# Expert stage of a streaming encoder step: the order in which a token list's entries are laid on the partitions

## The chip, the cores and the metric

The kernel runs on one core of a Trainium2 chip. The metric is the device time of one execution in microseconds. The kernel before was run three times: 1291.88, 1288.03 and 1289.56 us, median 1289.56 us. One more execution was taken with the hardware profiler; all rows below come from it.

## What is computed

The program is one layer of an encoder over 1024 prompt rows and 32 sample rows of width 1024: projections, two kinds of attention, an output projection, and then a mixture of 32 gated experts. Only the mixture bears on this change. Each of the 1056 rows picks one of four groups and two of the eight experts in it, so there are 2112 pairs of a row and an expert:

```python
g_sel = jnp.argmax(g_logits, axis=-1)
e_in = jnp.take_along_axis(e_logits, g_sel[:, None, None], axis=1)[:, 0]
top_v, top_i = lax.top_k(e_in, TOP_K)                       # TOP_K = 2
w2 = jax.nn.softmax(top_v, axis=-1) * p_g
idx = g_sel[:, None] * EXP_PER_GROUP + top_i
gates = jnp.einsum('ske,sk->se', jax.nn.one_hot(idx, N_EXPERTS), w2)
a = jnp.einsum('sd,edf->sef', hs, w_gate)                   # 1024 -> 256, for each expert
b = jnp.einsum('sd,edf->sef', hs, w_up)
act = jax.nn.silu(a) * b * gates[:, :, None]
return jnp.einsum('sef,efd->sd', act, w_down)               # 256 -> 1024
```

Working the routing out from the reference's own inputs gives how many rows each expert gets: between 37 and 107, 66 on average. These counts are used below. In the kernel's order of experts (four fixed ones, then 14 of the two middle groups by falling count, "busy", then 14 of the other two groups, "calm") they are 69, 70, 37, 47; busy 101, 94, 84, 78, 75, 74, 72, 67, 66, 61, 56, 54, 48, 46; calm 107, 92, 86, 80, 78, 73, 70, 63, 49, 47, 47, 42, 41, 38.

## The kernel before

Phase F (`phase_fr`) normalises and routes, and writes for each expert a list in device memory (`list_dram`, a region of rows for each expert): entry after entry, a row's number and its weight, 8 bytes together. Behind the last real entry stand padding entries whose number is out of bounds.

Phase G (`phase_g`) works in 23 blocks of 128 partitions. A block holds one expert (128 places), two experts with 64 places each, or 96 places of one expert and 32 of a fourth one that three such blocks share. `expert_blocks` makes this plan: for each block, pieces of (expert, first entry, places, first partition). Blocks 0, 1, 2 and 4 are the fixed experts; 3, 11, 13, 15 and 22 are pairs; 12 and 14 single experts; 5 to 10 and 16 to 21 are two and two groups of "four experts in three blocks".

For each block:
- a small DMA for each piece loads its entries of the list into `li[b]`, entry j on partition j of the piece. Lists 0 and 1 are loaded by SyncE at the end of phase F (L1879), the others by ScalarE (`list_in`, L2579), seven blocks' lists in a row at the start of phase G and then one block's list after each block, nine blocks ahead;
- GpSimd issues an indirect DMA that gathers the rows named in `li[b]` from `h2_dram` into one of four buffers (`gather`, L2389; the tiles `g_xg`, `early` and `o_s`), 4 KB for each partition; out-of-bounds entries are skipped;
- TensorE turns the rows (L2396), multiplies them by gate and up (L2404, 16 to 64 matmuls), turns the hidden rows (L2411) and multiplies them by down (L2419);
- VectorE scales the result by the entry's weight (L2632), and GpSimd issues an indirect DMA that adds the rows to the output `y` in device memory (`scatter`, L2383), 4 KB for each real entry. It waits for the scatter before it.

The weights, 3 MB for each of the other 28 experts, come in 1 MB DMAs issued by SyncE (`load_gate_up`, `load_down`, L2278 to L2284) into six slots; a slot is loaded again when TensorE has done with it. All DMAs of the core, whoever issues them, run on its 16 DMA engines. In `first_products` TensorE waits for the block's gate and up weights; the profile names no releaser for this wait and calls it "issue".

The order of the instructions on each engine is written out by hand in the program; no scheduler decides it.

Of the kernel before, what the change touches and what calls it, by code (L numbers as in the profile page):

```python
# [31 lines left out]
P = 128  # L32
D = 1024
KD = D // P
SEQ, DEC, PAST = 1024, 32, 2048
# [13 lines left out]
NG, EPG, NE, DE = 4, 8, 32, 256  # L49
# [1704 lines left out]
def phase_fr(nc, io, g):  # L1754

    with ExitStack() as stack:
# [85 lines left out]
        @block.sync  # L1842
        def _(sp):
            def rows_in(n):
                i, T, side = tile(n)
                if n >= 2:
                    sp.wait_ge(x2_done, n - 1)
                src = io["x_sample"] if side else io["x_prompt"][i * P:(i + 1) * P, :]
                sp.dma_start(xr[0:T, n % 2], src).then_inc(x_in[n % 2], 16)

            rows_in(0)
            rows_in(1)
            sp.dma_start(wr[:, :, 0:NG], io["w_rg"].rearrange("(k p) n -> p k n", p=P)).then_inc(r_in, 16)
            sp.dma_start(wr[:, :, GW:], io["w_re"].rearrange("(k p) n -> p k n", p=P)).then_inc(r_in, 16)
            sp.wait_ge(pad_done, 1)
            sp.dma_start(g.list_dram.rearrange("(p n) o -> p n o", p=P), pad[:]).then_inc(z_out, 16)
            for n in range(NT):
                i, T, side = tile(n)
                sp.wait_ge(x2_done, n + 1)
                sp.dma_start(io["y"][i * P:i * P + T, :], x2[0:T, n % 2]).then_inc(st_x2[n % 2], 16)  # L1860
                if n + 2 < NT:
                    rows_in(n + 2)
                sp.wait_ge(h2_done, n + 1)
                sp.dma_start(g.h2_dram[i * P:i * P + T, :], h2[0:T]).then_inc(st_h2, 16)
                if n in (1, 2, 6):
                    q = min(n - 1, 2)
                    load_gate_up(nc, io, g, sp, q * EPG, q, g.wgu_in[q])
                    load_down(nc, io, g, sp, q * EPG, q, g.wd_in[q])
            sp.wait_ge(pr_mm, NT)
            load_gate_up(nc, io, g, sp, 3 * EPG, 3, g.wgu_in[3])  # L1870
            load_down(nc, io, g, sp, 3 * EPG, 3, g.wd_in[3])
            sp.wait_ge(st_h2, 16 * NT)
            for b in range(2):
                sp.wait_ge(st_x2[b], 16 * len(range(b, NT, 2)))
            for b in range(2):
                sp.wait_ge(listed[b], 32 * len(range(b, NT, 2)))
            for b in range(2):
                row = b * EPG * REGION
                sp.dma_start(g.li[b][:], g.list_dram[row:row + P, :]).then_inc(g.li_in[b], 16)  # L1879

        @block.gpsimd
        def _(pool):
# [401 lines left out]
    engine.dma_start(g.w_down[b][:], io["w_down"][e].rearrange("(p k) n -> p k n", p=P)).then_inc(sem, 16)  # L2284


def expert_blocks():

    busy = lambda r: FIXED + r
    calm = lambda r: FIXED + RANKS + r  # L2290

    def whole(p):
        return [(p, 0, P, 0)]

    def halves(p, q):
        return [(p, 0, P // 2, 0), (q, 0, P // 2, P // 2)]

    def four_in_three(three, shared):
        w = 3 * P // 4
        return [[(p, 0, w, 0), (shared, i * DEC, DEC, w)] for i, p in enumerate(three)]  # L2300

    single = [whole(p) for p in (busy(0), calm(0))]
    paired = [halves(busy(r), calm(r)) for r in range(THREE, RANKS)]
    fours = []
    for r in range(WHOLE, THREE, 4):
        fours.append(four_in_three([busy(r), busy(r + 1), busy(r + 2)], calm(r + 3)))
        fours.append(four_in_three([calm(r), calm(r + 1), calm(r + 2)], busy(r + 3)))
    fixed = [whole(p) for p in range(FIXED)]
    blocks = fixed[0:3] + paired[0:1] + fixed[3:4] + fours[0] + fours[1] + paired[1:2] + single[0:1] + paired[2:3]
    return blocks + single[1:2] + paired[3:4] + fours[2] + fours[3] + paired[4:5]  # L2310


def phase_g(nc, io, g):

    with ExitStack() as stack:
# [7 lines left out]
        order = []  # L2323
        first_block, last_block = {}, {}
        for b in range(NB):
            for p, _, _, _ in blocks[b]:
                if p not in first_block:
                    order.append(p)
                    first_block[p] = b
                last_block[p] = b  # L2330
# [95 lines left out]

        def slots_of(b):

            unit = min(n for _, _, n, _ in blocks[b])
            return [place[p] for p, _, n, _ in blocks[b] for _ in range(n // unit)]  # L2430

        @block.sync
        def _(sp):
# [70 lines left out]
        @block.tensor  # L2504
        def _(pe):
            def first_products(b):
                for p, _, _, _ in blocks[b]:
                    pe.wait_ge(wgu_in[place[p]], 32 * nth[p] + 32)
                pe.wait_ge(xT_done, b + 1)
                if b:  # L2510
                    pe.wait_ge(hid_done, b)
                gate_up(b % 2, slots_of(b)).then_inc(gu_mm, 1)

            def rows_turned(b):
                pe.wait_ge(xg_in[b % ROWSETS], 16 * (b // ROWSETS) + 16)
                if b:
                    pe.wait_ge(xT_done, b)
                transposes(b % ROWSETS).then_inc(xT_mm, 1)

            def second_products(b):  # L2520
                for p, _, _, _ in blocks[b]:
                    pe.wait_ge(wd_in[place[p]], 16 * nth[p] + 16)
                pe.wait_ge(hT_done, b + 1)
                if b >= 2:
                    pe.wait_ge(y_done, b - 1)
                down(b % 2, slots_of(b)).then_inc(dn_mm, 1)

            def hidden_turned(b):
                pe.wait_ge(hid_done, b + 1)
                if b:  # L2530
                    pe.wait_ge(hT_done, b)
                hid_transposes().then_inc(hT_mm, 1)

            rows_turned(0)
            rows_turned(1)
            for b in range(NB + 1):
                if b == NB - 1:
                    second_products(b - 1)
                if b < NB:
                    first_products(b)  # L2540
                if b and b != NB - 1:
                    second_products(b - 1)
                if b + 2 < NB:
                    rows_turned(b + 2)
                if b < NB:
                    hidden_turned(b)

            def long_body(e, row, n):
                pe.wait_ge(l_xg, n * 16 + 16)
                transposes(0).then_inc(l_xT_mm, 1)  # L2550
                pe.wait_ge(l_xT, n + 1)
                pe.wait_ge(l_w, n * 48 + 48)
                gate_up(0, [0]).then_inc(l_gu, 1)
                pe.wait_ge(l_hid, n + 1)
                hid_transposes().then_inc(l_hT_mm, 1)
                pe.wait_ge(l_hT, n + 1)
                down(0, [0]).then_inc(l_dn, 1)

            long_lists(pe, long_body)

        @block.scalar
        def _(act):
            def squash():
                return nc.scalar.activation(sig[:], GU[:, 0:DE], ACT.Sigmoid)  # L2564

            def hidden_out(b):
                return nc.scalar.activation(hT[:, b], H[:, 0:FT * P].rearrange("p (k t) -> p k t", t=P), ACT.Copy)  # L2567

            AHEAD = 9
            experts = {r: r * EPG for r in range(FIXED)}  # L2570

            def expert(r):
                if r not in experts:
                    experts[r] = act.value_load(g.order[0:1, r:r + 1], min_val=0, max_val=NE - 1)
                return experts[r]

            def list_in(b):
                for r, row, n, at in blocks[b]:
                    act.dma_start(li[b][at:at + n, :], g.list_dram[bass.ds(expert(r) * REGION + row, n), :]  # L2579
                                  ).then_inc(li_in[b], 16)  # L2580

            act.wait_ge(xg_in[0], 16)
            for b in range(2, AHEAD):
                list_in(b)
            for b in range(NB):
                act.wait_ge(gu_mm, b + 1)
                if b:
                    act.wait_ge(hid_done, b)
                squash().then_inc(sig_done, 1)
                act.wait_ge(hT_mm, b + 1)  # L2590
                if b >= 2:
                    act.wait_ge(dn_mm, b - 1)
                hidden_out(b % 2).then_inc(hT_done, 1)
                if b + AHEAD < NB:
                    list_in(b + AHEAD)

            def long_body(e, row, n):
                act.wait_ge(l_gu, n + 1)
                squash().then_inc(l_sig, 1)
                act.wait_ge(l_hT_mm, n + 1)  # L2600
                hidden_out(0).then_inc(l_hT, 1)

            long_lists(act, long_body)
# [238 lines left out]
```

## Time and profile before

| | us |
|---|---|
| median of three runs | 1289.56 (1288.03 to 1291.88) |
| the profiled execution, from its first to its last instruction | 1289.9 |
| TensorE (PE) busy in it | 1182.8 (92%) |
| VectorE (DVE) busy | 672.3 (52%) |
| ScalarE (ACT) busy | 356.3 (28%) |
| GpSimd (POOL) busy | 212.8 (16%) |
| bytes moved by DMA | 213.47 MB, 165 GB/s over the span |
| expert stage, from the landing of the first lists to the end | 970.5 to 1289.9 |

The span of the profiled execution lies 0.3 us above the median of the runs. The page cuts the span into 40 slices of 32 us and gives for each the busy share of each engine, the clock granted to TensorE, and the mean busy share of the 16 DMA engines. A stretch can be asked for the same numbers. The chain of work that ended last lists, in order of time, what each piece of the critical path was.

### The profile page before, as it was taken

What the parts mean: (1) busy time and instruction counts of PE and PEld (TensorE: products, weight loads), DVE (VectorE), ACT (ScalarE), POOL (GpSimd) and SP (SyncE); (2) the same over time, 40 slices, a digit from 0 to 9 for tenths busy, and PEclk for the clock granted to TensorE, in tenths of its full rate; (3) what the DMA queues carried; (4) which work ended last, traced back from release to release, by engine and by line L of the source; (5) the groups of instructions that cost most, each with busy time, mean ns of one, the idle gap of its engine ahead of it and who ended that gap; (6) DMA issues with size and microseconds to landing.
All of it is one profiled execution on the core that took longest, in us unless ns stands there. A gap on an engine that the chain in (4) does not pass through costs nothing. (4 is left out here: it accounts for less than half of the span.)

```text
span 1289.9 us, 19011 instructions
## 1 busy us (share of the span) xinstructions
PE 1182.8 (92%) x7174; PEld 662.3 (51%) x7175; DVE 672.3 (52%) x1313; ACT 356.3 (28%) x781; POOL 212.8 (16%) x250
## 2 busy tenths in 40 slices
PE   4999999999978997899999999899976999977995
PEld 1555555555543556666677776555543433332331
DVE  1255443554465884567777775544462554433443
ACT  1122222222222444265555553323320000000000
POOL 4000000000000002254443322011022212211111
PEclk9899999999998998889999999899977999988998
DMA  8721211111137871421111005362447999999993
GB/s 361 297 66 33 66 53 46 53 45 54 41 122 226 300 275 58 124 58 30 29 29 30 2 1 165 121 231 89 184 152 285 337 367 367 382 395 377 357 348 65
DMA packets 92834, 213.47 MB, mean 165 GB/s; under 512 B 20673, under 2 KB 54707, under 8 KB 77394
## 3 DMA queue, kind: packets, MB, share of 16 engines
q1 hardware_dynamic: 82258, 195.02, 41.1%
q0 software_dynamic: 7200, 17.33, 5.4%
q8 instruction: 53, 0.87, 0.3%
q10 hardware_dynamic: 3296, 0.02, 0.1%
q14 instruction: 27, 0.22, 0.1%
HBM read 185.03 MB, written 34.13 MB: 170 GB/s over the span
## 5 line engine op out<-in xcount | busy, mean ns | idle before, releaser
L2404 PE MATMUL g_GU<-w_gu,first_region 128*32 128x512 f32 (+2 forms) x656 | 143.0, 624 | 17.0 <-issue 17.0
L1921 PE MATMUL f_C<-first_region,oT 128*128 128x512 f32 x256 | 115.2, 603 | 0.0
L454 PE MATMUL U<-region,b_hT 128*128 128x512 f32 x256 | 112.3, 592 | 0.0
L2614 DVE TENSOR_TENSOR g_sig<-g_GU,g_sig 128x256 f32<-128x256 f32 x23 | 9.8, 425 | 165.8 <-ACT g_sig L2564 157.7
L1723 DVE TENSOR_TENSOR_SCAN region<-region,early 128x128 f32<-128x128 f32 (+7 forms) x64 | 88.6, 1404 | 6.3 <-POOL region L1530 6.3
L2404 PEld LDWEIGHTS g_GU<-w_gu,first_region 128*32 128x32 f32 (+2 forms) x656 | 43.2, 127 | 84.3 <-issue 83.4
L454 PE MATMUL b_UL<-region,b_hT 128*128 128x384 f32 (+1 forms) x256 | 76.5, 458 | 3.3 <-DMA region<-w_in 3.3
L1921 PEld LDWEIGHTS f_C<-first_region,oT 128*128 128x128 f32 x256 | 48.0, 193 | 54.3 <-issue 54.2
L454 PEld LDWEIGHTS U<-region,b_hT 128*128 128x128 f32 x256 | 47.5, 190 | 54.2 <-issue 54.0
L2383 POOL DMA_INDIRECT y<-oT,g_li x23 | 36.4, 1584 | 227.0 <-DVE oT L2632 133.8
L1592 PE MATMUL e_Z<-first_region,region 104*128 104x512 f32 (+3 forms) x192 | 70.8, 507 | 0.1
L2419 PE MATMUL g_Y<-w_down,early 128*32 128x512 f32 (+2 forms) x328 | 68.8, 594 | 0.7 <-ACT early L2567 0.7
L1538 POOL TENSOR_SCALAR region<-region,e_sm 128x128 f32<-128x128 f32 (+7 forms) x64 | 47.0, 745 | 130.1 <-DVE e_sm L1736 130.1
L454 PEld LDWEIGHTS b_UL<-region,b_hT 128*128 128x128 f32 x256 | 49.9, 196 | 31.1 <-issue 5.5
L1052 POOL MEMSET region<- 128x256 f32 x1 | 0.3, 311 | 375.2 <-POOLq L303 375.2
L1729 DVE TENSOR_REDUCE e_sm<-e_Z 128x1 f32<-128x128 f32 (+7 forms) x64 | 46.4, 745 | 21.7 <-PE e_Z L1592 20.8
L2564 ACT ACTIVATE g_sig<-g_GU 128x256 f32<-128x256 f32 x23 | 8.8, 383 | 175.3 <-PE g_GU L2404 175.3
L454 PE MATMUL b_U<-region,b_hT 128*128 128x512 f32 x128 | 56.3, 592 | 0.0
L1685 ACT ACTIVATE region<-e_Z,e_sm 128x128 f32<-128x128 f32 (+7 forms) x64 | 47.2, 749 | 11.5 <-DVE e_sm L1729 11.4
L2404 PE MATMUL g_GU<-first_region 128*32 128x512 f32 (+2 forms) x144 | 49.4, 594 | 0.0
L1592 PEld LDWEIGHTS e_Z<-first_region,region 104*128 104x128 f32 x192 | 34.0, 199 | 29.3 <-issue 26.2
L1663 ACT ACTIVATE region<-e_Z 128x128 f32<-128x128 f32 (+7 forms) x64 | 38.1, 649 | 34.8 <-PE e_Z L1574 34.8
(489 smaller groups left out, 2160.2 us busy)
## 6 DMA issues: line engine op xcount, KB each, us to landing
w_gu<-w_gate SPq DMA_DIRECT2D x21, 1024.0 KB
w_gu<-w_up SPq DMA_DIRECT2D x21, 1024.0 KB
w_down<-w_down SPq DMA_DIRECT2D x21, 1024.0 KB
region<-w_ada SPq DMA_DIRECT2D x16, 1024.0 KB, 7.0
region<-w_in SPq DMA_DIRECT2D x3, 2048.0 KB, 17.5
oT<-w_gate SPq DMA_DIRECT2D x6, 1024.0 KB
oT<-w_up SPq DMA_DIRECT2D x6, 1024.0 KB
oT<-w_down SPq DMA_DIRECT2D x6, 1024.0 KB, 20.2
```

Of the source, the lines that this page charges most:

```text
L454: end = nc.tensor.matmul(dst[0:T, 0:c1 - c0], lhsT=hT[:, k, 0:T], rhs=g.w_in[:, k, c0:c1], start=k == 0, stop=k == KD - 1)
L1538: nc.gpsimd.tensor_scalar(part, part, sm[:, n % 2, 4 + hh:5 + hh], 1.0, ALU.mult, ALU.mult).then_inc(scaled, 1)
L1592: end = nc.tensor.matmul(Z[:, hh, at + c:at + c1], lhsT=g.q_hidden[:, b, h, :], rhs=g.kT_hidden[:, h, c:c1], start=True, stop=True)
L1663: nc.scalar.activation(stick[:, n % 2, hh, 0:W], Z[:, hh, at:at + W], ACT.Tanh, scale=0.5 * SB_SCALE).then_inc(tanh_done, 1)
L1685: nc.scalar.activation(w[:, hh, to:to + W], Z[:, hh, at:at + W], ACT.Exp, bias=sm[:, n % 2, hh:hh + 1], accum_out=sm[:, n % 2, 2 + hh:3 + ...
L1723: nc.vector.tensor_tensor_scan(back, back, least, 1.0, ALU.mult, ALU.max).then_inc(scan_done, 1)
L1729: nc.vector.tensor_reduce(sm[:, n % 2, hh:hh + 1], Z[:, hh, at:at + (t + 1) * P], AX.X, ALU.max, negate=True).then_inc(max_done, 1)
L1921: end = nc.tensor.matmul(C[n % 2][:, c * 512:(c + 1) * 512], lhsT=g.oT[:, i, k, :], rhs=wo[:, k, c * 512:(c + 1) * 512], start=k == 0, sto ...
L2383: nc.gpsimd.indirect_dma_start(out=io["y"][:, :], in_=rows, in_offset=None, out_offset=bass.IndirectOffsetOnAxis(ap=li[:, 0:1], axis=0), b ...
L2404: end = nc.tensor.matmul(GU[h * n:h * n + n, :], lhsT=xT[:, b, k, h * n:h * n + n], rhs=wgu[s][:, :, k, :], start=k == 0, stop=k == KD - 1 ...
L2419: end = nc.tensor.matmul(Y[b][h * n:h * n + n, c * 512:(c + 1) * 512], lhsT=hT[:, b, k, h * n:h * n + n], rhs=wd[s][:, k, c * 512:(c + 1) ...
L2614: mark(nc.vector.tensor_tensor(sig[:], GU[:, 0:DE], sig[:], ALU.mult))
```

## The change

The pieces get one more number, the step between the list's entries that they take, and every list is read through a new helper.

```diff
+def list_rows(g, row, first, step, n):
+
+    rows = g.list_dram[bass.ds(row, n * step), :].rearrange("(r q s) c -> s q r c", r=8, s=step)
+    return rows[first]
...
     def whole(p):
-        return [(p, 0, P, 0)]
+        return [(p, 0, 1, P, 0)]
 
     def halves(p, q):
-        return [(p, 0, P // 2, 0), (q, 0, P // 2, P // 2)]
+        return [(p, 0, 1, P // 2, 0), (q, 0, 1, P // 2, P // 2)]
 
     def four_in_three(three, shared):
         w = 3 * P // 4
-        return [[(p, 0, w, 0), (shared, i * DEC, DEC, w)] for i, p in enumerate(three)]
+        return [[(p, 0, 1, w, 0), (shared, i, 3, DEC, w)] for i, p in enumerate(three)]
...
-                for r, row, n, at in blocks[b]:
-                    act.dma_start(li[b][at:at + n, :], g.list_dram[bass.ds(expert(r) * REGION + row, n), :]
+                for r, first, step, n, at in blocks[b]:
+                    act.dma_start(li[b][at:at + n, :], list_rows(g, expert(r) * REGION, first, step, n)
                                   ).then_inc(li_in[b], 16)
```

The load of lists 0 and 1 at the end of phase F goes through `list_rows` too, with step 1 and 128 entries. For a piece with n places the helper reads the list as 8 stretches of n/8 entries and takes the first of each stretch, then the second of each, and so on: entry j goes to partition 8 * (j mod n/8) + j div (n/8) of its piece. Consecutive entries land eight partitions apart. A shared expert with places in three blocks gives its entries 0, 3, 6, ... to the first of them, 1, 4, 7, ... to the second and 2, 5, 8, ... to the third; before, they got entries 0 to 31, 32 to 63 and 64 to 95.

The destination of each load is the same; the source is read as (n/8) x 8 x 2 numbers, so its outermost dimension is 16, 12, 8 or 4 where it was 128, 96, 64 or 32. No instruction is added, taken away or moved. On ScalarE, at the start of phase G (lists of block 2, of the two halves of block 3, and of block 4; the ISA rows are register work for the expert's address), stood before:

```order
L2579 DMA g_li<-list_dram 128x2
L2574 TENSOR_LOAD order
L2574 ISA x2
L2579 ISA
L2579 DMA g_li<-list_dram 64x2
L2574 TENSOR_LOAD order
L2574 ISA x2
L2579 ISA
L2579 DMA g_li<-list_dram 64x2
L2579 DMA g_li<-list_dram 128x2
```

and now stands, in the same place:

```order
L2584 DMA g_li<-list_dram 128x1x2
L2579 TENSOR_LOAD order
L2579 ISA x2
L2584 ISA
L2584 DMA g_li<-list_dram 64x1x2
L2579 TENSOR_LOAD order
L2579 ISA x2
L2584 ISA
L2584 DMA g_li<-list_dram 64x1x2
L2584 DMA g_li<-list_dram 128x1x2
```

Only the form of the DMAs differs, and the line numbers by five.

## Rows read from the trace of the kernel before

**Rows 1.** The page: DMA share (tenths) and GB/s in 40 slices of 32 us

```profile
DMA  8721211111137871421111005362447999999993
GB/s 361 297 66 33 66 53 46 53 45 54 41 122 226 300 275 58 124 58 30 29 29 30 2 1 165 121 231 89 184 152 285 337 367 367 382 395 377 357 348 65
```

**Rows 2.** Stretches of the expert stage: busy by engine, granted clock, DMA share, GB/s

```profile
core 0: us, PE busy (x) PEld busy (x) DVE busy (x) ACT busy (x) POOL busy (x), PEclk, DMA share, GB/s
1000.00:1040.00 40.00, 40.00 (x158) 18.33 (x160) 21.39 (x31) 2.68 (x7) 7.92 (x6) 1.00 0.93 334
1040.00:1180.00 140.00, 129.63 (x845) 49.60 (x838) 56.64 (x85) 8.05 (x21) 28.86 (x22) 0.95 1.02 379
...
1139.90:1144.00 4.10, 4.00 (x10) 1.38 (x12) 0.00 (x0) 0.00 (x0) 0.00 (x0) 0.50 1.02 357
```

**Rows 3.** The waits between 1100 and 1240 us, TensorE: total, times, longest

```profile
PE g_GU L2404 <- issue: 17.0, 4, 7.3
```

**Rows 4.** The chain that ended last, in the expert stage: start, us, what

```profile
968.79 1.69 DMA g_li<-list_dram
...
1120.87 6.87 PE g_GU L2404 x16
...
1132.65 7.34 issue
1139.99 9.68 PE g_GU L2404 x32
...
1166.21 3.03 issue
1169.24 8.72 PE g_GU L2404 x32
...
1182.72 5.17 issue
1187.89 9.61 PE g_GU L2404 x64
...
1202.41 7.00 PE g_GU L2404 x64
...
1225.94 1.46 issue
```

**Rows 5.** The last scatter (84 rows, nothing else moves), in stretches of 0.3 us

```profile
1284.90:1285.20 0.30, 0.00 (x0) 0.00 (x0) 0.00 (x0) 0.00 (x0) 0.00 (x0) 0.50 1.02 205
1285.20:1285.50 0.30, 0.00 (x0) 0.00 (x0) 0.00 (x0) 0.00 (x0) 0.00 (x0) 0.50 0.95 164
1285.50:1285.80 0.30, 0.00 (x0) 0.00 (x0) 0.00 (x0) 0.00 (x0) 0.00 (x0) 0.50 0.50 83
1285.80:1286.10 0.30, 0.00 (x0) 0.00 (x0) 0.00 (x0) 0.00 (x0) 0.00 (x0) 0.50 0.37 69
1286.10:1286.40 0.30, 0.00 (x0) 0.00 (x0) 0.00 (x0) 0.00 (x0) 0.00 (x0) 0.50 0.35 68
1286.40:1286.70 0.30, 0.00 (x0) 0.00 (x0) 0.00 (x0) 0.00 (x0) 0.00 (x0) 0.50 0.34 68
```

**Rows 6.** The first two gathers (69 and 70 rows), same columns

```profile
974.00:975.00 1.00, 0.00 (x0) 0.00 (x0) 0.00 (x0) 0.00 (x0) 0.63 (x1) 0.50 0.57 201
```

**Rows 7.** Around the gather of block 2, TensorE and VectorE in order of time

```profile
990.57 1.16 PE L2396 MATMUL g_X<-ident,early 128*128 128x128 f32 x8 [0.73 <-DMA early<-h_dram,g_li]
991.57 0.40 PE L2411 MATMUL g_H<-ident,g_hid 128*128 128x128 f32 x2
...
1002.11 1.05 PE L2396 MATMUL g_X<-ident,o_s 128*128 128x128 f32 x8
```

```profile
990.75 0.42 DVE L2615 TENSOR_TENSOR g_hid<-g_GU,g_sig 128x256 f32<-128x256 f32 x1
```

**Rows 8.** GpSimd in order of time: gathers of blocks 2 to 4, first scatter

```profile
981.47 0.99 POOL L2389 DMA_INDIRECT early<-h_dram,g_li  x1 [6.84 <-DMA g_li<-list_dram]
...
985.60 0.99 POOL L2389 DMA_INDIRECT o_s<-h_dram,g_li  x1 [2.16 <-DMA g_li<-list_dram]
989.17 0.99 POOL L2389 DMA_INDIRECT g_xg<-h_dram,g_li  x1 [2.57 <-DMA g_li<-list_dram]
...
1004.70 1.62 POOL L2383 DMA_INDIRECT y<-oT,g_li  x1 [6.51 <-DVE oT L2632]
```

**Rows 9.** The page: DMA queue of ScalarE's list loads: packets, MB, share

```profile
q10 hardware_dynamic: 3296, 0.02, 0.1%
```

More of the change, by code:

```diff
@@ L1877, in _ @@
             for b in range(2):
-                row = b * EPG * REGION
-                sp.dma_start(g.li[b][:], g.list_dram[row:row + P, :]).then_inc(g.li_in[b], 16)
+                sp.dma_start(g.li[b][:], list_rows(g, b * EPG * REGION, 0, 1, P)).then_inc(g.li_in[b], 16)
         @block.gpsimd
@@ L2325, in phase_g @@
         for b in range(NB):
-            for p, _, _, _ in blocks[b]:
+            for p, *_ in blocks[b]:
                 if p not in first_block:
@@ L2427, in slots_of @@
         def slots_of(b):
-            unit = min(n for _, _, n, _ in blocks[b])
-            return [place[p] for p, _, n, _ in blocks[b] for _ in range(n // unit)]
+            unit = min(n for _, _, _, n, _ in blocks[b])
+            return [place[p] for p, _, _, n, _ in blocks[b] for _ in range(n // unit)]
         @block.sync
@@ L2506, in first_products @@
             def first_products(b):
-                for p, _, _, _ in blocks[b]:
+                for p, *_ in blocks[b]:
                     pe.wait_ge(wgu_in[place[p]], 32 * nth[p] + 32)
@@ L2520, in second_products @@
             def second_products(b):
-                for p, _, _, _ in blocks[b]:
+                for p, *_ in blocks[b]:
                     pe.wait_ge(wd_in[place[p]], 16 * nth[p] + 16)
```

## The prediction, written before the changed kernel was run

> **What bounds the kernel now.** The page's slices come first, because the change touches DMAs alone. Before the expert stage the DMA engines are mostly idle; from slice 31 to slice 39 they stand at 9 tenths and move 337 to 395 GB/s [rows 1]. Next come stretches of that stage. From 1000 to 1040 us the DMA share is 0.93 and TensorE has no gap; from 1040 to 1180 us the share is 1.02, so that all 16 DMA engines have work all the time, and TensorE is busy 129.63 of 140 us [rows 2]. The waits say where the rest goes: TensorE stands four times, 17.0 us in all, ahead of gate-and-up products [rows 3], and the code has a wait for weights there. The chain gives the places: 7.34 us at 1132.65 (block 13), 3.03 us (block 15), 5.17 us (block 16) and 1.46 us at 1225.94 (block 19) [rows 4]. The products behind the three long waits take 9.68, 8.72 and 9.61 us where the others take 6.87 to 7.00: after the first of them the granted clock is 0.50 up to 1144 us, 1.2 of 2.4 GHz [rows 2]. Another 2.7 + 1.7 + 2.6 = 7.0 us. So up to 24 us of this stage hang on DMA, and outside these places it runs at TensorE's pace.
>
> A wait for weights ends when the last of the 16 DMA engines has done its part. A weight load gives each engine the same; a gather or a scatter doesn't, since it skips padding. What counts is how many rows fall to the engine that gets most, in each block: its "depth". Lowering that is the only way in which this change can reach those 24 us.
>
> **Which engine moves which partition.** Nothing names it, but the last scatter shows it, because nothing else moves then. Block 22 holds 46 rows on partitions 0 to 45 and 38 rows on 64 to 101. Had each engine eight consecutive partitions, 46 = 5 x 8 + 6 and 38 = 4 x 8 + 6 rows would keep 11 engines busy, a share of 0.69 to the end. The rows show 1.02 and 0.95, then 0.50, 0.37, 0.35, 0.34 [rows 5]: all 16 engines, then six (0.375). That fits groups of four partitions, dealt in turn to eight engines in each half of the partitions: 12 groups in the first half are one for each engine and a second for four, 10 groups in the second half are one each and a second for two; 4 + 2 = 6. An engine then has partitions 4e to 4e + 3 and the four that lie 32 further on. The first gathers, 69 and 70 rows, run at a share of 0.57 [rows 6]: some nine engines of 16.
>
> The Trainium skill says the same of the shares ("DMA: Bandwidth & Descriptors", The descriptor swizzle: four consecutive partitions and the four that lie 32 on). It speaks against this change as much as the rows do; the sum doesn't need it.
>
> **The change part by part.** (1) *Entries eight partitions apart.* With 128 places, entry j lands on partition 8 (j mod 16) + j div 16. Entries 0 to 63 fill the first four places of each eight, so they all lie in every second group of four, and these groups go to every second engine. Those eight engines get 8 rows each, the other eight only what is over 64. Before, entries 0 to 63 lay on the first 64 partitions: eight engines with 8 rows each. The idle engines are other ones, the depth is 8 both times. The same count for 64 places: entries 0 to 31 fill four engines with 8 each. For 96 places entries 0 to 47 fill every second group in the same way. Going through the 23 blocks with the lists' lengths, the depth is 8 in all of them before, and 8 in 21 after; only blocks 2 (37 rows) and 4 (47 rows) fall to 6. Over the stage the deepest engine has 184 rows before and 180 after, where an even spread would give 132.
>
> What those two blocks are worth: block 2's gather is on the path at the start, since TensorE stands 0.73 us for it [rows 7]. But the hidden rows that are turned behind it at 991.57 come from VectorE at 990.75 + 0.42 = 991.17, so at most some 0.4 us can be won; I take 0.3. A scattered row costs a DMA engine: 69 GB/s at a share of 0.37 is 69 / (0.37 x 16) = 11.7 GB/s for one engine, 4096 bytes in 0.35 us [rows 5]. A gathered row: 201 / (0.57 x 16) = 22 GB/s, 0.19 us [rows 6]. Block 4's scatter falls behind 1040 us, where the engines are saturated: 2 x 0.35 = 0.7 us from each later wait for weights. The other rows (block 2's gather and scatter, block 4's gather) fall ahead of 1040 us, where TensorE doesn't wait; if they count after all it is 2 x 0.35 + 4 x 0.19 = 1.5 us more. Taken: -0.7, bounds 0 and -2.2.
>
> (2) *The shared expert's entries in turn.* Of 78, 75, 49 and 66 entries, the blocks get 26/26/26, 25/25/25, 17/16/16 and 22/22/22 where they got 32/32/14, 32/32/11, 32/17/0 and 32/32/2. This evens out blocks' totals, but the 96 other places already put 8 rows on some engine in each of the 12 blocks. 0 us.
>
> (3) *The list loads.* Each still carries its n entries of 8 bytes, read with a stride. The first two lists landed in 1.69 us [rows 4] with eight entries an engine; that stays. For the shorter loads the trace can't show what a source with an outermost dimension of 12, 8 or 4 does. If each were spread over that many engines, the first four would hold 16 list entries for a pair or four-in-three block where they held 8: 17 blocks x 8 = 136 more. Priced by the queue's own row, 0.1% (0.05 to 0.15) of 16 x 1289.9 us over 3296 packets is 3 to 9 ns each [rows 9], so 0 to +1.2 us on one of the deepest engines; eight of the 17 blocks' lists are loaded after 1040 us, 64 x 6 ns = 0.4 us, which I take. At the start the lists arrive 3.6 to 4.1 us apart, at 981.47, 985.60 and 989.17 [rows 8]. If a pair's takes twice that, block 3's gather starts at 989.4; a gather there takes 9.05 us at most (981.47 to 990.52), and TensorE wants it at 1002.11 [rows 7], so it may start as late as 993. The first scatter stands behind the gathers on GpSimd's queue and would come at some 1009 for 1004.70 [rows 8]; VectorE wants its end two blocks on, after 1025. Nothing on the path.
>
> The skill does state a rule on this ("DMA: Bandwidth & Descriptors", Why a DMA increments its semaphore by 16 and not by 1): the number of engines is the largest one up to 16 that divides the slowest dimension of both sides, and it is the lowest-numbered ones. By it the loads run on 16, 12, 8 and 4 engines; no row of this trace shows it. The sum by it is the +0.4 us taken, and without it 0.
>
> (4) *More engines at the same depth.* One engine had 8 rows in every block; now all of every second one have, but for two blocks. A wait for the last of eight is a little longer than one for the last of three or four: 0 to +1 us, I take +0.3, about one row's packet.
>
> Sum: -0.3 - 0.7 + 0 + 0.4 + 0.3 = -0.3 us on a span of 1289.9 us, which lies 0.3 us above the median of the runs. The forecast is 1289.3 us: no change that can be measured. About 0.3%, 3.9 us, is what a measurement of this kernel can tell from none.
>
> **The rivals.** *A: the rows are evened out after all.* If each engine took eight consecutive partitions in gathers and in scatters under load, transposed lists would give each the ceiling of rows/16. By block 19's weights the deepest engine would save 14 scattered rows of blocks 4 to 15 (96 to 82) and 19 gathered rows of blocks 10 to 22 (104 to 85): 14 x 0.35 + 19 x 0.19 = 8.5 us, all of it out of the 24 us. That is 1289.6 - 8.5 = 1281 us, and some 1278 if shorter waits also spare the clock. For it: depth is what the waits hang on. Against it: the six engines of rows 5, which eight consecutive partitions can't give. *B: slower, by the list loads.* Same spreading as in (3), but each entry costs an engine more than its packet time, since it is a read of its own that stands between 8 KB packets. It decides from 3.9 / 64 = 0.06 us an entry on. The dearest row is the 1.69 us of a load with eight entries deep, 0.21 us each with all latency in it [rows 4]; half-way, 0.12 us, gives 64 x 0.12 = +8 us, 1297 us; at the bound it is 1303. Against it: 3 to 9 ns [rows 9].
>
> **How the numbers follow.** The forecast holds 0.82, rival A 0.09, rival B 0.09. Within the forecast the bounds of the parts are -0.4 - 2.2 = -2.6 and +1.2 + 1.0 = +2.2 us; with 2 us for the spread of the runs (1288.03 to 1291.88) that is 1285.2 to 1293.8. This leaves out the two rivals, 0.18, so it is the range. Of the forecast's 0.82, some 0.04 lie beyond the 3.9 us on the fast side and 0.03 on the slow side: faster 0.13, same 0.75, slower 0.12.
>
> **What would show it.** In the profile after: the last scatter falls from a share of 1 to about 0.5 (eight engines) half-way instead of 0.37, and ends as late; the waits for weights at blocks 13, 15, 16 and 19 stay, 15 to 18 us in all; the wait of 0.73 us for block 2's gather is gone. Rival A shows as a last scatter of even share to the end and as waits under 10 us. Rival B shows as longer waits and list loads that land much later. The number of packets on the list loads' queue tells of (3): it falls if loads end on fewer engines. What would make the prediction wrong above all is that the engines are dealt the partitions in another way under load than in the last scatter.

## The result: 1301.34 us for 1290.72, slower by 0.8%

| | median (lowest to highest) | ratio to before, 95% interval | span profiled |
|---|---|---|---|
| before, beside it | 1290.72 us (1288.03 to 1292.56) | 1 | 1289.9 us |
| changed kernel | 1301.34 us (1299.28 to 1302.86) | 1.0081 (1.0061 to 1.0100) | 1301.2 us |

The forecast was 1289.3 us, no change, with a range up to 1293.8. The time lies 12.0 us above the forecast and outside the range. The profiled execution of the changed kernel took 1302.85 us, one of its slower ones, with a span of 1301.2 us. The two spans lie 0.1 and 0.8 us below the medians and can stand for the runs.

The stage still ends as it did: the chain that ended last runs through TensorE, and its waits for weights have hardly moved. The waits and the two windows of [rows 2] come first; in a row of waits stand the engine, the line and what it waits for, then the total, the times and the longest. First the waits between 1100 and 1240 us of the changed kernel, then two stretches of it with busy time by engine, granted clock, DMA share and GB/s:

```profile
PE g_GU L2409 <- issue: 18.1, 4, 6.8
```

```profile
1000.00:1040.00 40.00, 40.00 (x127) 18.68 (x126) 17.30 (x25) 2.69 (x7) 7.30 (x6) 0.94 0.70 246
1040.00:1180.00 140.00, 129.80 (x858) 50.36 (x858) 60.70 (x88) 8.45 (x22) 30.35 (x24) 0.97 1.01 377
```

Beside [rows 3] that is 18.1 us for 17.0, and beside [rows 2] the saturated 140 us are the same stretch again: 129.80 us of TensorE for 129.63, share 1.01 for 1.02. What differs is the stretch ahead of it. Only 127 products ran from 1000 to 1040 us where 158 did, at a granted clock of 0.94 where it was 1.00. Nearly all of the 11 us is lost before 1040 us, as the chain shows. Pieces of the chain of the changed kernel (start, us, what), to be read against [rows 4]:

```profile
975.34 0.69 ACTq L2584
...
1000.37 9.22 PE g_GU L2409 x16
...
1143.39 6.78 issue
1150.17 9.55 PE g_GU L2409 x32
...
1176.25 3.42 issue
...
1192.89 5.44 issue
```

The wait at block 13 begins at 1143.39 for 1132.65, 10.74 us later; nearly all of the loss is there by then. From 975.34 to 997 us the chain leads through something that [rows 4] doesn't have: ACTq, ScalarE's own queue, at the line that loads the lists. ScalarE in order of time (start, us, engine, line, operation, count, idle time before and its releaser), of the kernel before:

```profile
975.66 11.41 ACTq L2579 DMA_DIRECT2D g_li<-list_dram  x12
987.10 1.28 ACT L2564 ACT_TABLE_LOAD   x1 [26.19 <-issue]
989.88 0.38 ACT L2564 ACTIVATE g_sig<-g_GU 128x256 f32<-128x256 f32 x1 [1.49 <-PE g_GU L2404]
```

and of the changed kernel:

```profile
975.34 21.65 ACTq L2584 DMA_DIRECT2D g_li<-list_dram  x12
997.02 1.28 ACT L2569 ACT_TABLE_LOAD   x1 [36.70 <-issue]
998.32 0.38 ACT L2569 ACTIVATE g_sig<-g_GU 128x256 f32<-128x256 f32 x1
```

ScalarE issues twelve list loads, for blocks 2 to 8, ahead of the stage's first sigmoid. They took 11.41 us; they take 21.65 us. Before, ScalarE had done with them and with its table and then waited 1.49 us for TensorE. Now the sigmoid stands behind them without any gap. Who waits for that sigmoid is in TensorE's own rows of the changed kernel:

```profile
989.35 1.06 PE L2401 MATMUL g_X<-ident,early 128*128 128x128 f32 x8
999.67 0.70 PE L2416 MATMUL g_H<-ident,g_hid 128*128 128x128 f32 x2 [9.26 <-DVE g_hid L2620]
```

TensorE stands 9.26 us for the hidden rows that VectorE makes from this sigmoid. The gate-and-up products of block 1, right behind, take 9.22 us for 6.87: a window of the changed kernel shows the clock there.

```profile
1000.30:1005.00 4.70, 4.70 (x7) 1.89 (x6) 0.45 (x1) 0.38 (x1) 0.99 (x1) 0.50 0.47 158
```

The granted clock is 0.50, 1.2 of 2.4 GHz, behind a gap of 9.26 us; before, without the gap, these products began at 991.81. In all: the sigmoid comes 27.38 us after the start of the first gather (970.94 to 998.32) where it came 18.57 us after it (971.31 to 989.88), 8.81 us more; 9.22 - 6.87 = 2.35 us for the clock; waits of 18.1 for 17.0, 1.1 us. That is 12.3 us. The slowed products behind the long waits give 0.7 back (9.55 + 8.45 + 9.34 for 9.68 + 8.72 + 9.61), and the first gather starts 0.37 us sooner in the span (970.94 for 971.31). So 11.2 us, where the spans differ by 11.3 and the medians by 10.6.

What one load costs the queue is in the rows of the tile: shortest, median and longest issue in ns, first and last start. Of the kernel before, then of the changed one:

```profile
L2579 ACTq DMA_DIRECT2D g_li<-list_dram x38: 322/362/998, 975.7 to 1156.4; - x38
```

```profile
L2584 ACTq DMA_DIRECT2D g_li<-list_dram x38: 580/1116/1319, 975.3 to 1167.5; - x38
```

The number of loads is the same, 38; only the way in which the source is read has changed. The issues are not the whole of it. Between the loads of the start ScalarE reads the number of the next expert eight times, and these reads take longer too. Before, then changed, same columns:

```profile
L2574 ACTq TENSOR_LOAD <-order x8: 275/290/479, 976.1 to 986.0; - x8
```

```profile
L2579 ACTq TENSOR_LOAD <-order x8: 476/605/820, 976.1 to 995.0; - x8
```

Added up over the instructions of the traces, the twelve issues take 12.43 us for 4.74 and the eight reads 5.01 for 2.49: 7.7 and 2.5 us of the 10.24 by which the row of twelve grew.

### The profile page after: what moved, and what is told of

Its sections match the earlier page's. It is cut to its first block and busy times, and to the rows that moved or that the text cites. A ratio compares the mean times of both kernels' runs of the same rounds, so it can differ in the third digit from the quotient of the medians.

```text
span 1301.2 us, 19011 instructions
## 1 busy us (share of the span) xinstructions
PE 1184.0 (91%) x7174; PEld 663.3 (51%) x7175; DVE 672.3 (52%) x1313; ACT 356.3 (27%) x781; POOL 212.8 (16%) x250
## 5 line engine op out<-in xcount | busy, mean ns | idle before, releaser
L2409 PE MATMUL g_GU<-w_gu,first_region 128*32 128x512 f32 (+2 forms) x656 | 144.7, 625 | 18.1 <-issue 18.1
```

The source lines that it names most:

```text
L2409: end = nc.tensor.matmul(GU[h * n:h * n + n, :], lhsT=xT[:, b, k, h * n:h * n + n], rhs=wgu[s][:, :, k, :], start=k == 0, stop=k == KD - 1 ...
```

## The experiments

The theory (Q): the loss is ScalarE's time for issuing list loads, ahead of the first sigmoid. Its first rival (D) is the prediction's rival B: the loads' entries hold up the DMA engines between weights. The second (M) is the new mapping itself, by which blocks draw more engines and rows. The kernel before was run again beside the experiments: its median is 1290.2 us beside e2, e3, e4 and e7, and 1290.3 us beside e5, e6, e8 and e9.

**e2: six blocks' lists ahead instead of nine.** The changed kernel, with the loads of blocks 2 to 5 only ahead of the first sigmoid (lists 0 and 1 come from SyncE as before); the others follow one block at a time. The loads, their mapping and their entries are the same.

```diff
-            AHEAD = 9
+            AHEAD = 6
```

> The changed kernel, but ScalarE loads the lists of blocks 2 to 5 (6 DMAs) ahead of its first sigmoid, not those of blocks 2 to 8 (12 DMAs). Theory 1 (the strided list loads take ScalarE's queue 0.6 to 1.3 us each, where they took 0.3 to 0.6, and twelve of them stand ahead of the first sigmoid): the six end at about 985.6 us, the first sigmoid starts at 989.9 again, behind TensorE's first products, and the time is that of the kernel before, 1289 to 1292 us. Theory 2 (the entries fall on few DMA engines, so lists, gathers or weights arrive late): the same entries on the same engines, the time stays at 1300 to 1303 us.

Measured: 1291.62 us (1288.88 to 1293.94), ratio 1.0011 (1.0000 to 1.0023). The loss is gone. ScalarE of this kernel, in order of time:

```profile
973.71 10.25 ACTq L2584 DMA_DIRECT2D g_li<-list_dram  x6
983.99 1.28 ACT L2569 ACT_TABLE_LOAD   x1 [25.31 <-issue]
987.88 0.39 ACT L2569 ACTIVATE g_sig<-g_GU 128x256 f32<-128x256 f32 x1 [2.61 <-PE g_GU L2409]
```

Six loads take 10.25 us, ScalarE waits for TensorE again, and the sigmoid comes 18.58 us after the start of the first gather (969.30), as in the kernel before. All 38 loads are there, as dear as in the changed kernel (median 1114 ns), and more of them fall where the DMA engines are saturated: the last one starts at 1203.5 us. If entries on the DMA engines were the cost (D), or the mapping (M), this kernel would be no faster than the changed one.

**e7 and e8: the delay alone, in the kernel before.** Small copies on ScalarE into a tile that nothing reads, between the loads and the first sigmoid; lists and mapping stay those of before.

```diff
+        idle = m.sb("g_idle", [P, 36 * 32])
...
+            for n in range(36):
+                nc.scalar.activation(idle[:, n * 32:n * 32 + 32], g.gate_m[:, 0, 0:32], ACT.Copy)
```

> The kernel before with its lists as they were, and 36 small copies on ScalarE (some 0.23 us each, 8 us together) between the list loads and the first sigmoid. Theory 1: a late first sigmoid alone costs what the change cost; the sigmoid starts at about 996 to 998 us, the first products behind it run at the lower clock, and the time is 1298 to 1302 us. Theory 2: ScalarE's time is not what counts, 1289 to 1292 us.

The 36 copies took about half of what was meant, 4.40 us, and the time stayed under the 1298 to 1302 us expected. So the second run has 76 copies, of 16 columns each.

> As the run with 36 small copies ahead of the first sigmoid, with 76 of them; one took 0.12 us there, so the sigmoid starts at 987.1 + 76 x 0.12 + 1.3 = 997.5 us, 0.8 us ahead of the changed kernel's 998.3. Theory 1: the products behind it start 7.7 us late and run some 2 us longer at the lower clock, 1299 to 1301.5 us with lists as before. If it stays at the 1294.7 us of the short delay, a late sigmoid explains only half of the loss.

Measured: e7 1294.74 us (1292.07 to 1296.41), ratio 1.0032 (1.0020 to 1.0045); e8 1300.20 us (1298.09 to 1303.43), ratio 1.0076 (1.0058 to 1.0095). ScalarE of e8:

```profile
987.37 8.14 ACT L2587 ACTIVATE g_idle<-gate_m 128x16 f32<-128x16 f32 x76 [25.98 <-issue]
...
996.81 0.38 ACT L2565 ACTIVATE g_sig<-g_GU 128x256 f32<-128x256 f32 x1
```

| | first gather to first sigmoid | later than before | block 1's products | time over before |
|---|---|---|---|---|
| before | 18.57 us | | 6.87 us | |
| e7 | 21.52 us | 2.95 us | 8.56 us | 4.5 us |
| e8 | 25.11 us | 6.54 us | 8.59 us | 9.9 us |
| changed kernel | 27.38 us | 8.81 us | 9.22 us | 10.6 us |

A late first sigmoid is enough to make the kernel before slower by about as much as the changed one. The first 3 us cost 4.5 because the gap also brings the granted clock down for the products behind it (0.63 from 994.40 to 999.00 us in e7; 8.56 us for 6.87, +1.7). In e8 the delay and the clock explain 6.54 + 1.72 = 8.3 of the 9.9 us; its profiled execution also waits 19.3 us for weights, 2.3 more than before, and is the slowest of its four runs, so how much of the rest is scatter stays open.

The waits for weights don't take the delay back in any of the three, because the loads of weights start later too. The first weight load that waits for block 0's down products to free a slot stands in SyncE's rows; of the kernel before, then of the changed one:

```profile
1002.31 0.33 SPq L2284 DMA_DIRECT2D w_down<-w_down  x1
```

```profile
1013.06 0.33 SPq L2283 DMA_DIRECT2D w_down<-w_down  x1
```

That is 10.75 us later, as much as the wait at block 13 moved. In e7 this load starts at 1006.45 and in e8 at 1010.92.

**e6: the shared expert's entries in turn, alone.** The kernel before; the three 32-place pieces of a shared expert read entries 0, 3, 6, ..., 1, 4, 7, ... and 2, 5, 8, ..., everything else as it was.

```diff
-        return [[(p, 0, w, 0), (shared, i * DEC, DEC, w)] for i, p in enumerate(three)]
+        return [[(p, 0, w, 0), (shared, i, DEC, w)] for i, p in enumerate(three)]
...
+                    if at == 3 * P // 4:
+                        src = g.list_dram[bass.ds(expert(r) * REGION, 3 * n), :].rearrange("(q s) c -> s q c", s=3)[row]
```

> One part of the change alone: a shared expert's entries go to its three blocks in turn, all lists untransposed. The source of these loads keeps 32 as its outermost dimension, so by theory 1 their issue stays near 0.33 us and the first sigmoid at 990 us; the depth of rows stays 8. 1289 to 1292 us, waits for weights 16 to 19 us. If it takes half of the 10 us, the loss is in the shared pieces and not in the transposed lists.

Measured: 1289.74 us (1287.76 to 1293.20), ratio 1.0000 (0.9990 to 1.0011). The tile's row of this kernel:

```profile
L2582 ACTq DMA_DIRECT2D g_li<-list_dram x38: 322/364/636, 974.6 to 1156.1; - x38
```

The 0 us of the prediction's part (2) stands, and a stride between 32 entries by itself doesn't make a load dear: the outermost dimension is still 32.

**e3: entries four partitions apart.** The changed kernel with one number changed; consecutive entries then land in successive groups of four partitions, which by [rows 5] are different engines.

```diff
-    rows = g.list_dram[bass.ds(row, n * step), :].rearrange("(r q s) c -> s q r c", r=8, s=step)
+    rows = g.list_dram[bass.ds(row, n * step), :].rearrange("(r q s) c -> s q r c", r=4, s=step)
```

> The changed kernel with entries four partitions apart (4 stretches of n/4 entries, outermost dimension 32, 24, 16 or 8). By the reading of the last scatter (groups of four partitions dealt to the DMA engines in turn) this evens out the rows: the deepest engine has 150 rows for 184, and by block 19's weights it is 12 to 19 rows of each kind less, 7.3 us. The late first sigmoid stays. Theory 1: 1301 - 7 to 9, and up to 1.5 us less if the issue of a load is dear only where its outermost dimension spreads over fewer than 16 engines (then the loads of 64 places take 0.6 us again): 1291 to 1295 us, waits for weights under 12 us for 18.1. If partitions were dealt to engines eight by eight, the waits would stay at 18 us and the time at 1300.

Measured: 1288.99 us (1287.21 to 1292.25), ratio 0.9988 (0.9975 to 1.0001), 12.4 us faster than the changed kernel and hardly faster than before. Two things meet. The loads ahead of the first sigmoid, with the register work between them, still take 20.16 us for 21.65, the sigmoid comes 25.07 us after the first gather's start, 6.50 later than before, and block 1's products take 8.54 us: 6.50 + 1.67 = 8.2 us lost. Against that, the waits between 1100 and 1240 us of this kernel are

```profile
PE g_GU L2409 <- issue: 11.1, 4, 5.2
```

5.9 us less than [rows 3], and the products behind the long waits take 7.09 + 9.32 + 8.77 = 25.2 us for 28.0. Sum -0.5 us; the medians say -1.2. The run is 2 us faster than its expectation, which began at 1291: the waits and the products behind them gave more than the 7.3 us counted (beside the changed kernel 7.0 and 2.2 us).

**e4: four apart, six ahead.** Both edits.

> Both edits: entries four partitions apart, and only four blocks' lists ahead of the first sigmoid. Theory 1: the first sigmoid at 989.9 us as before, and waits for weights shorter by 7 us: 1281 to 1285 us, faster than both kernels. Theory 2: 1291 to 1295 us, no better than with nine blocks ahead.

Measured: 1282.02 us (1280.76 to 1285.10), ratio 0.9942 (0.9919 to 0.9964). This beats both kernels. Its waits between 1100 and 1240 us, then two pieces of its chain:

```profile
PE g_GU L2409 <- issue: 13.6, 3, 5.5
```

```profile
1126.90 2.72 issue
1129.62 7.09 PE g_GU L2409 x32
```

Against e2, which differs in the mapping alone, the medians are 9.6 us apart. The waits are 13.6 for 19.3 us (-5.7), the products behind the three longest 25.5 for 27.2 us (-1.7), and the start of the stage to the first sigmoid 16.41 for 18.58 us (-2.2: the first gather takes 3.50 us for 4.39, block 0's products 7.52 for 8.80). That adds up to the 9.6, but such agreement is partly luck: the profiled spans differ by 10.5 us, 1.3 of them ahead of the first gather (967.96 for 969.30), and the waits of kernels at the same depth scatter by 2.5 us (16.8 to 19.3 us). Its last scatter shows what the mapping does, in stretches of 0.3 us with the columns of [rows 5]; first e4, then the changed kernel:

```profile
1275.10:1275.40 0.30, 0.00 (x0) 0.00 (x0) 0.00 (x0) 0.00 (x0) 0.00 (x0) 0.50 0.99 178
1275.40:1275.70 0.30, 0.00 (x0) 0.00 (x0) 0.00 (x0) 0.00 (x0) 0.00 (x0) 0.50 1.00 191
1275.70:1276.00 0.30, 0.00 (x0) 0.00 (x0) 0.00 (x0) 0.00 (x0) 0.00 (x0) 0.50 0.80 150
1276.00:1276.30 0.30, 0.00 (x0) 0.00 (x0) 0.00 (x0) 0.00 (x0) 0.00 (x0) 0.50 0.28 41
```

```profile
1296.00:1296.30 0.30, 0.00 (x0) 0.00 (x0) 0.00 (x0) 0.00 (x0) 0.00 (x0) 0.50 0.98 110
...
1296.90:1297.20 0.30, 0.00 (x0) 0.00 (x0) 0.00 (x0) 0.00 (x0) 0.00 (x0) 0.50 0.57 109
...
1297.80:1298.10 0.30, 0.00 (x0) 0.00 (x0) 0.00 (x0) 0.00 (x0) 0.00 (x0) 0.50 0.55 109
```

Four apart, all engines carry nearly the same and the scatter is over at once. Eight apart, about half of them carry the rest alone, for longer. The groups of four that the prediction read from [rows 5] hold for gathers and scatters in the loaded part too: counted with them, the deepest engine has 150 rows over the stage where it had 184 before and 180 in the changed kernel, worth 7.3 us up to block 19 by the prediction's prices of a row, and the waits with their slowed products gave 7.4 between e2 and e4 and 7.3 between e2 and e9. The step is clear of the scatter: the seven kernels whose depth is nearly 8 throughout (184 or 180 rows) waited 16.8 to 19.3 us, the three evened ones 11.1, 13.6 and 14.0.

**e5: six ahead in the kernel before.** The same one-line edit as e2, so that its worth isn't put down to the wrong part.

> The kernel before with four blocks' lists ahead of the first sigmoid for seven, nothing else. Control for the two runs with that edit: before, ScalarE was free at 988.4 us and the sigmoid waited for TensorE until 989.88, so this should give nothing, 1289 to 1291.5 us. If it is faster by 2 us or more, part of what the other two runs gained is not the cure of a late sigmoid.

Measured: 1290.62 us (1289.74 to 1295.30), ratio 1.0006 (0.9991 to 1.0020). With loads of 0.37 us ScalarE's queue is not on the path there: the first sigmoid waits for TensorE in the kernel before, and with fewer loads ahead it only waits longer (7.12 us for 1.49). What e2 wins back is what the strided loads had cost, and the gain of e4 over before is the mapping's.

**e9: every load on an outermost dimension of 16 or a multiple, six ahead.** Groups chosen by size: 128 places four apart, 96 places six apart, 64 four apart, 32 two apart.

```diff
-    rows = g.list_dram[bass.ds(row, n * step), :].rearrange("(r q s) c -> s q r c", r=8, s=step)
+    rows = g.list_dram[bass.ds(row, n * step), :].rearrange("(r q s) c -> s q r c", r={P: 4, 3 * P // 4: 6, P // 2: 4, DEC: 2}[n], s=step)
...
-            AHEAD = 9
+            AHEAD = 6
```

> Lists transposed with 4 stretches for 128 and 64 places, 6 for 96 and 2 for 32, so that the outermost dimension is 32 or 16 for all, and six blocks ahead. If the issue of a list load is dear where the outermost dimension doesn't hold 16, all loads now take 0.55 to 0.7 us (1.28 us for 96 places and 1.15 for 32 before), against theory 1b, that the stride alone makes them dear, by which 96 places stay at 1.28 us. The rows are nearly as even (153 on the deepest engine, 46.7 us by block 19 for 46.1): 1280 to 1284 us, equal to the best one.

Measured: 1282.79 us (1280.63 to 1283.99), ratio 0.9942 (0.9929 to 0.9956), the same as e4. The tile's row of e9:

```profile
L2584 ACTq DMA_DIRECT2D g_li<-list_dram x38: 552/590/687, 974.5 to 1197.3; - x38
```

No load takes more than 687 ns any more. It brings no time over e4, since with six ahead the queue is off the path in both (the sigmoid waits 4.55 and 2.90 us for TensorE); it tells what makes a load dear. The single issues at the start of the stage, each one row of ScalarE in order of time (piece of 64, of 96 and of 32 places), of the changed kernel:

```profile
977.22 1.16 ACTq L2584 DMA_DIRECT2D g_li<-list_dram  x1
...
982.17 1.32 ACTq L2584 DMA_DIRECT2D g_li<-list_dram  x1
...
984.44 1.17 ACTq L2584 DMA_DIRECT2D g_li<-list_dram  x1
```

of e3:

```profile
973.73 0.61 ACTq L2584 DMA_DIRECT2D g_li<-list_dram  x1
...
977.04 1.38 ACTq L2584 DMA_DIRECT2D g_li<-list_dram  x1
...
979.33 1.22 ACTq L2584 DMA_DIRECT2D g_li<-list_dram  x1
```

and of e9:

```profile
976.35 0.60 ACTq L2584 DMA_DIRECT2D g_li<-list_dram  x1
...
979.66 0.62 ACTq L2584 DMA_DIRECT2D g_li<-list_dram  x1
...
980.99 0.61 ACTq L2584 DMA_DIRECT2D g_li<-list_dram  x1
```

The outermost dimensions of the three are 8, 12 and 4 in the changed kernel; 16, 24 and 8 in e3; 16, 16 and 16 in e9. The piece of 64 falls from 1.16 to 0.61 us when it goes from 8 to 16. The piece of 96 stays at 1.38 with 24 and falls to 0.62 with 16. So it isn't the number as such, nor how far apart the entries lie (12 or 24 apart the piece of 96 is dear, 16 apart it isn't): a load is cheap where the outermost dimension lets it run on 16 engines.

The other way round it doesn't always hold. The pieces of 32 places of blocks 6 and 7 in the changed kernel, on 4 engines as well, are nearly as cheap as in e9:

```profile
988.32 0.70 ACTq L2584 DMA_DIRECT2D g_li<-list_dram  x1
...
991.72 0.66 ACTq L2584 DMA_DIRECT2D g_li<-list_dram  x1
```

Eight of its twelve pieces of 32 places take 0.66 to 0.70 us, the other four 1.14 to 1.19. The cheap ones start within 0.5 us of the end of the load before; ahead of the dear ones stands the read of an expert's number, and they start 0.9 us or more behind it. e2, e3 and e4 show the same split. Why the spacing matters, no run shows.

## Why the prediction was wrong

**The step that failed is (3), the list loads.** It priced what each load does once it is under way: its landing, its entries on the DMA engines. It never priced the issuing. The document ahead of it says that ScalarE loads seven blocks' lists in a row at the start of the stage, and the queue's own time was to be had from the trace of before: 11.41 us for twelve loads, with 1.49 us of slack behind them. A term "twelve loads by an unknown more each, minus the slack" was missing. From 1.49 / 12 = 0.12 us a load the slack is used up, and with the 2.35 us for the clock (3.9 + 1.49 - 2.35) / 12 = 0.25 us a load decide the case. It was 10.24 / 12 = 0.85 us with the reads between the loads, and 10.24 - 1.49 = 8.75 us is the delay of 8.81 us. "Nothing on the path" was true for GpSimd's gathers, which step (3) followed (block 3's gather was put at 989.4 and began at 989.13), and false for ScalarE, on whose queue the moved cost lay. GpSimd's rows of the changed kernel show both:

```profile
989.13 1.00 POOL L2394 DMA_INDIRECT o_s<-h_dram,g_li  x1 [7.79 <-DMA g_li<-list_dram]
...
1015.45 1.62 POOL L2388 DMA_INDIRECT y<-oT,g_li  x1 [10.91 <-DVE oT L2637]
```

The first scatter was put at some 1009 us and began at 1015.45, behind the late products.

**Rival B had the side and the operation, not the mechanism.** It expected 1297 to 1303 us, from entries at 0.06 to 0.21 us each on a DMA engine. The time fell in that interval, but e2 keeps every entry and loses the cost, and e8 has no strided load at all and shows it. The agreement in size is chance.

**The mapping (1) was right.** The last scatter falls to about half of the engines (share 0.55) and is no shorter (8.1 us from its issue to the end for 8.0); the waits at blocks 13, 15, 16 and 19 stay, 18.1 us where 15 to 18 were given. Block 2's wait of 0.73 us is gone, but it is swallowed by the 9.26 us that follow. Nothing of the taken -0.3 and -0.7 can be told from noise. Rival A, the rows evened out, is false for this change; e3 and e4 show that evening them out, with four for eight, is worth about what A's price of a row gives.

**The shared entries (2)** were put at 0, and e6 measures 0. **Part (4)**, more engines at the same depth, was +0.3; e2 and e5 differ in the change alone, with the queue off the path in both: ratios of 1.0011 and 1.0006, 0.6 us apart, with intervals by which it can be some 2.5 us more or less. So (1) to (4) together, the queue's time left out, are small, as the forecast's -0.3 has it; the single terms aren't settled further.

**The packets of the list loads' queue** fell, as step (3) allowed. Of the changed kernel and of e3, e9 being back at 3296:

```profile
q10 hardware_dynamic: 3024, 0.02, 0.1%
```

```profile
q10 hardware_dynamic: 3152, 0.02, 0.1%
```

Beside [rows 9] that is 272 and 144 fewer. One packet for each entry and one for each engine that takes part fit the number before: 512 + 640 + 1152 + 384 = 2688 entries (4 loads of 128 places, 10 of 64, 12 of 96 and 12 of 32) and 38 x 16 = 608 make 3296. By this count 10 loads of 64 places on 8 engines, 12 of 96 on 12 and 12 of 32 on 4 take away 80 + 48 + 144 = 272. For e3, 64 places on 16 engines, 96 on 12 and 32 on 8 give 48 + 96 = 144. So the spreading that step (3) could only suppose is there; its +0.4 us was the wrong thing to take from it.

## What to carry to other kernels

A DMA costs twice: on the DMA engines and on the queue that issues it (here 0.34 to 1.38 us for each list load). For each edit of an access pattern, count the issues that stand in a row ahead of something that others wait for, and take their time and the slack behind them from that queue's own rows. Deal the rows of an indirect transfer to partitions by the groups in which the engines take them (here fours): an order that looks spread out over the partitions can still fall on half of the engines.

## What the hardware showed that was not expected

The issue time of a small load on ScalarE's queue depends on its source's form. Loads of 64, 96 and 32 places with consecutive entries took 0.56, 0.37 and 0.34 us in the kernel before, in the places whose rows stand under e9:

```profile
977.04 0.56 ACTq L2579 DMA_DIRECT2D g_li<-list_dram  x1
...
980.19 0.37 ACTq L2579 DMA_DIRECT2D g_li<-list_dram  x1
...
981.27 0.34 ACTq L2579 DMA_DIRECT2D g_li<-list_dram  x1
```

With two source dimensions and all 16 engines it is 0.60, 0.62 and 0.61 us (e9), so the form itself costs 0.04 to 0.27 us. On 8, 12 and 4 engines it is 1.16, 1.32 and 1.17 us, another 0.55 to 0.7. The extra isn't in proportion to the engines left out: 12 engines cost more than 4. It is nearly absent (0.66 to 0.70 us) where a load on 4 engines follows within 0.5 us of another, as shown under e9. The reads of an expert's number behind such loads lengthen too: 0.48 us and more in the changed kernel, where all but the first take 0.27 to 0.28 us at the start of e9.

By the packets counted above, the trace agrees with the Trainium skill ("DMA: Bandwidth & Descriptors", Why a DMA increments its semaphore by 16 and not by 1) on the number of engines: the largest up to 16 that divides the slowest dimension of both sides. The page says too that the issuing sequencer itself writes the rest of the 16 when fewer engines take part. Whether this writing is what costs the extra isn't shown by any run here. What the runs do show: in the changed kernel, e2, e3, e4 and e9 no load on 16 engines takes over 0.69 us, and every load of 96 places on 12 engines and of 64 places on 8 takes 1.10 us or more.
